# One kernel, eight cores: the first feed-forward's down weights cast from DRAM to DRAM during the first gate

## The reference

```python
D_MODEL = 1024; BATCH = 16; SEQ = 2048; D_FF = 2816
def swiglu(x, w_gate, w_up, w_down):
    return (jax.nn.silu(x @ w_gate) * (x @ w_up)) @ w_down
...
    h = swiglu(rms_norm(x, ffn1_pre_g[l]), ffn1_w_gate[l], ffn1_w_up[l], ffn1_w_down[l])
    x = x + 0.5 * rms_norm(h, ffn1_post_g[l])
    h = hybrid_mixer(rms_norm(x, mix_pre_g[l]), w_in[l], ...)
    x = x + rms_norm(h, mix_post_g[l])
    h = swiglu(rms_norm(x, ffn2_pre_g[l]), ffn2_w_gate[l], ffn2_w_up[l], ffn2_w_down[l])
    x = x + 0.5 * rms_norm(h, ffn2_post_g[l])
```

## Time and profile before

| | |
|---|---|
| time, median of 3 runs (lowest to highest) | 3015.21 us (3010.27 to 3282.29) |
| profiled execution: time, span of its slowest core | 3003.53 us, 3002.0 us |
| spans of the eight cores | 2973.8 to 3002.0 us |
| TensorE, VectorE, ScalarE, GpSimd busy | 94%, 55%, 49%, 26% |
| DMA queues' packet time, share of 16 engines: GpSimd's, SP's, ScalarE's | 31.3%, 17.6%, 6.6% |
| moved by DMA | 433.54 MB |

### The profile page before, as it was taken

One profiled execution on the slowest core, in us unless ns is written; L12 is line 12 of the kernel. 1 busy time (PEld: TensorE's weight loads), 2 busy tenths in 40 slices (PEclk: granted clock), 3 DMA queues, 4 the chain that ended last, 5 costly groups with the idle time before them and its releaser, 6 DMA issues.

```text
span 3002.0 us, 59376 instructions; the slowest of 8 cores (2973.8 to 3002.0 us)
## 1 busy us (share of the span) xinstructions
PE 2816.8 (94%) x18494; PEld 1468.5 (49%) x18494; DVE 1649.1 (55%) x3054; ACT 1467.9 (49%) x2642; POOL 767.5 (26%) x1028
## 2 busy tenths in 40 slices
PE   6989899999999988999989999999999998999997
PEld 2433344445666645554434466665555443444443
DVE  4330742465655566664867656556766585541523
ACT  2312332335667766775543366667777554113112
POOL 1313332332122112002762101111000374123123
PEclk9999899999999999999999999999999999999998
DMA  7998987496454364224886614223312587645636
GB/s 148 171 176 193 230 211 221 125 222 174 90 138 96 86 135 96 57 66 131 248 241 185 177 47 122 72 64 101 86 47 65 140 261 227 174 158 147 169 98 180
DMA packets 189775, 433.54 MB, mean 144 GB/s; under 512 B 25024, under 2 KB 42688, under 8 KB 188864
## 3 DMA queue, kind: packets, MB, share of 16 engines
q0 software_dynamic: 64704, 218.67, 31.3%
q1 hardware_dynamic: 82048, 143.42, 17.6%
q10 hardware_dynamic: 42720, 67.65, 6.6%
HBM read 407.89 MB, written 99.09 MB: 169 GB/s over the span
## 4 chain that ended last, share of the span: by engine, by line
PE 75%; DMA 8%; DVE 7%; issue 4%; ACT 4%; POOL 1%; ACTq 0%; DVEq 0%; SPq 0%; POOLq 0%
PE ps L821 34%; PE ps L711 17%; PE ps L920 6%; PE ps L1084 4%; PE ps L1061 4%; PE ps L1097 3%; PE ps L941 3%; PE ps L1120 2%; DMA xr<-x_s 2%; DVE xr L683 2%; DMA qk<-c_aug 1%; DMA xr<-xT 1%; DMA wsl<-wd 1%; DVE xnf L681 1%; ACT Pt L1102 1%
## 5 line engine op out<-in xcount | busy, mean ns | idle before, releaser
L821 PE MATMUL ps<-xnh,wsl 128*128 128x512 bf16 x5632 | 1324.9, 384 | 35.5 <-DVE sg L830 11.6
L821 PEld LDWEIGHTS ps<-xnh,wsl 128*128 128x128 bf16 x5632 | 542.4, 99 | 649.3 <-issue 90.6
L711 PE MATMUL ps<-hT,wsl 128*128 128x512 bf16 x2816 | 662.4, 384 | 30.3 <-DMA wsl<-wd 17.5
L830 DVE SCALAR_TENSOR_TENSOR sg<-sg,ps 128x512 f32<-128x512 f32 x352 | 239.7, 685 | 508.7 <-ACT sg L828 476.4
L828 ACT ACTIVATE sg<-ps 128x512 f32<-128x512 f32 x352 | 208.7, 596 | 537.1 <-PE ps L821 493.6
L553 POOL TENSOR_TENSOR rst<-rst,sq 128x512 f32<-128x512 f32 x276 | 340.5, 1242 | 397.8 <-ACT sq L551 391.8
L711 PEld LDWEIGHTS ps<-hT,wsl 128*128 128x128 bf16 x2816 | 272.0, 99 | 339.0 <-issue 59.7
L1069 ACT ACTIVATE Pt<-ps 128x512 bf16<-128x512 f32 x576 | 307.0, 578 | 201.9 <-PE ps L1061 157.0
L158 POOL DMA_DIRECT2D wsl<-wgu_s x286 | 155.6, 545 | 952.9 <-PE ps L821 523.8
L1102 ACT ACTIVATE Pt<-ps 128x512 bf16<-128x512 f32 (+3 forms) x640 | 312.0, 536 | 100.8 <-PE ps L1097 44.7
L835 DVE SCALAR_TENSOR_TENSOR hT<-sg,ps 128x512 bf16<-128x512 f32 x352 | 238.2, 683 | 121.1 <-PE ps L821 119.6
(11 more groups left out here) (78 smaller groups left out, 2481.5 us busy)
## 6 DMA issues: line engine op xcount, KB each, us to landing
wsl<-wd_s POOLq DMA_DIRECT2D x232, 352.0 KB, 4.7
wsl<-wgu_s POOLq DMA_DIRECT2D x286, 256.0 KB, 4.0
xr<-x_s SPq DMA_DIRECT2D x256, 256.0 KB, 6.2
xr<-xT SPq DMA_DIRECT2D x164, 256.0 KB, 9.9
x_s<-xr ACTq DMA_DIRECT2D x128, 256.0 KB, 5.3
wsl<-wgu POOLq DMA_DIRECT2D x66, 256.0 KB, 7.7
outT<-xr ACTq DMA_DIRECT2D x64, 256.0 KB, 4.5
winw<-win POOLq DMA_DIRECT2D x48, 256.0 KB, 5.0
```

What stands on the lines that cost most here:

```text
L711: S.op(PE, lambda e, k=k, w_fn=w_fn, pb=pb: e.matmul(ps[pb][:], w_fn(k), rhs(k), start=(k == 0), stop=(k == nk - 1)), reads=w_bufs + [rhs_ ...
L821: S.op(PE, lambda e, wi=wi, pb=pb, kc=kc, tl=tl: e.matmul(ps[pb][:], wsl[wi][:, kc * 128:(kc + 1) * 128], xnh[:, kc, tl * TT:(tl + 1) * TT ...
```

## The change

The down weights of the first feed-forward are no item that casts or is kept any more: all 32 items of every job load from `wd_s`. A new task, `cast_first`, spawned right behind `loader`, waits 30 us of planned time and then issues 16 DMAs on GpSimd's queue, one each 9.5 us of planned time: each casts one half block of `wd` (1408 columns) from fp32 into bf16, DRAM to DRAM. All of them write `B_pc`, and each the `B_wdb` of its half, on which the loads of that half wait. The loads' order and slots are the same.

```diff
@@ -736,7 +736,7 @@
                     items.append((cast, keep, wgu_d[fi][f][:, cs], wgb_d[fi, f][:, cs], B_wgb[fi][f][gu], NKC * 128))
             for tl in range(2):
                 for d in range(NKC):
-                    cast, keep = ji == 0 and tl <= d % 2, ji == 0 and tl == d % 2
+                    cast = keep = False
                     for hf in range(2):
                         cs = slice(hf * HF * 128, (hf + 1) * HF * 128)
                         items.append((cast, keep, wd_d[fi][d][:, cs], wdb_d[fi, d][:, cs], B_wdb[fi][d][hf], HF * 128))
@@ -770,6 +770,15 @@
                 B = B_wsl[i % NWS]
                 S.dma(SP, kept, wsl[i % NWS][:, 0:n], reads=[B], writes=[bf], track=B_wst[i % NWS])
             return i % NWS
+
+        def cast_first():
+
+            yield ("d", 30.0)
+            for d in range(NKC):
+                for hf in range(2):
+                    cs = slice(hf * HF * 128, (hf + 1) * HF * 128)
+                    S.dma(POOL, wdb_d[0, d][:, cs], wd_d[0][d][:, cs], writes=[B_pc, B_wdb[0][d][hf]], track=B_pc)
+                    yield ("d", 9.5)
 
         def cast_second():
 
@@ -800,6 +809,7 @@
             y_tile1 = (ysb_h, [[B_hT[YF + 2 * k][0], B_hT[YF + 2 * k + 1][0]] for k in range(NKC)])
             spawn_pre(0)
             drv.spawn(loader())
+            drv.spawn(cast_first())
             yield ("d", 0.0)
             for ji, (s, fi, h) in enumerate(jobs):
                 base = ji * n_items
```

## The result

The changed kernel takes 3024.59 us (median of 12 runs) where the kernel before takes 3013.23: a ratio of 1.0051, interval 1.003 to 1.0072. It is slower by 9 to 22 us; 3000 was forecast, a gain of 13. (Ratios leave out disturbed runs; where single cores of a profile ran at a lower clock, the text says which cores are used.)

What follows compares the result with a forecast made beforehand. TensorE was taken as the bound, so only its starved first down phase could give much: -19.5 removal, +5 gate stall, +1 late casts made -13.5 us, about 3001 from the median, named 3000; range 2982 to 3033.

Steps and rivals of the forecast that it cites:

- the price of the removal: First job's down phase: without casting loads and stores it falls from 99.5 to 80 us, gaining 19.5, at most 22.9.
- where the new waits would stand: First job's gate: a short wait of TensorE for gate weights was to stand near 130 us.
- The DMA share from 65 to 190: Sign in the first job's gate: the DMA engines' share was to rise from 0.87 to about 1.0.
- The traffic weighed against a row: Gate stretch: 43.1 MB at 304 GB/s need 142 us for 125, an excess of 17, or 7 beyond the cover.
- I take 5 us of stall in the gate: First job's gate: TensorE loses 5 us to casts delaying gate loads, from 0 to 16.
- the 12 us that I had named as the sign of it: First job's gate: growth by over 12 us would show the prediction wrong.
- The price of a cast: DMA engines: one cast takes 2.3 us of all 16, between 2.2 and 3.7.
- 24 free: Gate from 65 to 190: 16 us idle plus savings on down loads and stores leave 24 us of DMA time.
- 10 us of cover: Gate loads: issued 17.4 us before use and landing in 6.7, so about 10 us of delay would be absorbed.
- 1 us for late casts: First job's down phase: casts landing after their loads are due cost 1 us, from 0 to 5.
- rival b: GpSimd's queue: casts wait for each other and delay gate loads, so slower, about 3035 us; chance 0.16.
- rival a: First job's gate: DMA engines lack time for casts, so 12 to 20 us are paid; about 3012; chance 0.2.

Runs made afterwards that it cites:

- e2: Changed kernel without any casts; the first feed-forward's down items load as many bytes from the gate weights' scratch, so other weights are multiplied; ratio to before 0.9981.
- e4: Changed kernel with each cast tracked by its own buffer and the statistics matmuls of job 1's x tiles planned 15 us later; ratio to before 1.0007.
- e8: Changed kernel with own tracker per cast, late statistics matmuls and every cast issued twice, the second into unused scratch; no ratio given, first gate 234.9 us.
- e5: Changed kernel with its single tracking buffer kept and only job 1's statistics matmuls planned 15 us later; one run, 3006.0 us.
- e1: Changed kernel with each cast tracked by its own buffer, so none waits for the one before; no timed ratio, first gate 174.3 us on cores 4 to 7.
- e6: Changed kernel with only even d cast in the gate; odd d casts its loads and stores them in the down phase as before; one run, 2996.4 us.
- e9: Changed kernel with only even d cast in the gate, own tracker per cast and statistics matmuls planned 15 us later; ratio to before 0.9992.
- the control: Kernel before the change, with only the statistics matmuls of job 1's x tiles planned 15 us later; ratio to before 0.9997.

## Why the prediction was wrong

**Right.** The start of the casts (64.21 us on core 0 for 66.5), an untouched startup, the price of the removal (19.5 forecast, 19.4 in e2), and where the new waits would stand: for gate weights, the first long one ending at 116 to 123 us rather than at 130. The DMA share from 65 to 190 was to rise to about 1.0: 0.95 in the changed kernel, 1.01 in e4 (core 0, to the gate's end). The traffic weighed against a row held best: the excess of 17 us at the 304 GB/s of the earlier trace rows is what the gate paid, 17.4 and 15.7. Counting as there the bytes that the packets moved, a cast's fp32 side included, from 65 to the gate's end, the cores of the changed kernel ran at 286 to 304 GB/s, those of e4 at 302 to 312, of e8 at 303 to 320; the kernel before, not full, at 231 to 239. *The Trainium skill, "HBM Reference", section "Specifications (TRN2)": by its 358 GB/s the casts would have fitted; the gates measured here, full by their DMA share, stayed below that, so the row decides.*

**Wrong, first: "I take 5 us of stall in the gate".** Two terms made it too small, and the gate passed the 12 us that I had named as the sign of it. The price of a cast was taken at 2.3 us, from a casting load of another stage; in the full gate it is 3.0 (e8), and the trace of the kernel before had the nearer row, its own casting loads in the gate at 2.8. 13.5 casts are then 41 us against 24 free, a backlog of 17. And I let 10 us of cover stand against a backlog. It is paid nearly in full: 17.4 us in the changed kernel, 13.2 in e4. In e8 32 x 3.0 - 24 = 72, and 5 for the 1.4 MB more that SP's queue moved in the longer gate, stand against 80 measured; as the 3.0 comes from e8 too, this is a check of the sum rather than a second proof. Price and cover as corrected give the gate; either alone gives 7 us.

**Wrong, second: 1 us for late casts.** The waits for bf16 down weights are 6.2 us (mean of the cores; 0 to 5 was the bound), and the down phase is 8.1 us longer than in e2 (85.7 for 77.6). Casts that land in 9.7 us, each waiting for the last, slip from 209 to 223, as rival b said they would, and e5 against e4, one execution of each, puts 3.8 us on that chain. By phases the sum is -19.4 + 17.4 + 8.1 - 2.4 (the next gate) = 3.7 us. That 3024.59 lies between 2982 and 3033 says little, for that range held rivals of either sign.

So rival a, with "12 to 20 us" paid in the gate, was the mechanism; rival b described what a trace shows on top of it, and e1 shows that taking its wait away moves the stall and saves nothing in the gate.

**Open.** Whether the DMA engines' own time or the memory behind them is the limit in the gate: price and traffic both give its length, and no run here tells them apart. What lengthens the next gate in e6 and e9. Some 5 us between the phases of the profiles and the timed ratio, and why of e2's 13 to 19 us at the third job only 4 to 12 reach the end; the control's 4.9 us is of that size.

## What to carry to other kernels

Work moved ahead of its stage is free only if the resource it uses is free there: a DMA share of 0.87 left 24 us for 41 us of casts, and TensorE paid the difference. Take the price of a transfer from a row of the stage that it moves into: 2.2 us from the down phase, 2.8 in the gate. A waiting engine in the trace may be only the messenger: take its wait away by another buffer, and see whether the time comes back or the stall moves. To price an operation that has no row, issue it twice; the second time is all cost.

## What the runs showed that I had not expected

A cast from DRAM to DRAM cost 3.0 us of all 16 DMA engines for 704 KB read in the full gate, 2.7 of it in its own packets, and the casting load of the same bytes into SBUF 2.8 there but 2.2 from 190 to 220: the stage made the difference, and not the target. A plain copy of 352 KB cost 1.8 in the gate. The DMA view counts a cast's KB on its bf16 side, so 165 GB/s in the row of a full gate stood for some 290 GB/s of memory traffic. And the casts' wait for each other, 65.6 us of GpSimd's time, cost the gate nothing measurable: 168.8 us with it, 168.1 without.
